# Sparse attention: keys and values multiplied once and copied to the other partitions by VectorE; compression's products alternate between TensorE's column groups

## The reference

```python
def nsa_mixer(h, w_in, w_out, pos_k, pos_v, k_w1, k_w2, v_w1, v_w2):   # G=4 groups, R=4 heads each, dh=64
    q, k_c, v_c, k_s, v_s, k_w, v_w, gates = jnp.split(h @ w_in, NSA_SPLITS, axis=-1)
    def compress(kv, pos, w1, w2):          # 15 windows of 32 tokens, stride 16
        blk = kv[:, cmp_idx] + pos[None, None, :, None, :]
        blk = jnp.moveaxis(blk, 3, 2).reshape(B_, n_cmp, G, CMP_BLOCK * dh)
        return jax.nn.gelu(blk @ w1) @ w2
    kc = compress(k_c, pos_k, k_w1, k_w2)
    vc = compress(v_c, pos_v, v_w1, v_w2)
    o_cmp = softmax(q kc) vc                # masked: windows that have ended
    o_slc = softmax(q k_s) v_s              # selected blocks: with 256 tokens all of them, causal
    o_win = softmax(q k_w) v_w              # window of 512: causal
    o = gates[0] * o_cmp + gates[1] * o_slc + gates[2] * o_win
    return o.reshape(B_, S_, NSA_HEADS * dh) @ w_out
```

## Time and profile before

| | |
|---|---|
| median of 3 runs | 3059.75 us (3054.98 to 3066.94) |
| the profiled execution | 3071.72 us, its span 3069.8 us |
| PE busy | 2931.2 us, 95% of the span |
| DVE busy | 2096.6 us, 68% |
| ACT busy | 1472.3 us, 48% |
| DMA | 521.48 MB, mean 170 GB/s |
| first sparse layer | its first unit begins at 1687.94 us, its attention ends at about 1854 us |
| second sparse layer | 2678.32 to about 2844 us |

### The profile page before, as it was taken

How to read it: one execution, slowest core, us unless ns; L and a number is a source line. 1 busy time by engine, 2 the same in 40 slices (tenths; PEclk the granted TensorE clock), 3 DMA queues, 4 the chain that set the end, 5 groups by cost and what they waited for, 6 DMA issues and landing times.

```text
span 3069.8 us, 54616 instructions
## 1 busy us (share of the span) xinstructions
PE 2931.2 (95%) x23236; PEld 2602.9 (85%) x23236; DVE 2096.6 (68%) x3263; ACT 1472.3 (48%) x1965; POOL 149.0 (5%) x257
## 2 busy tenths in 40 slices
PE   6999999989999998999999999999999999999998
PEld 5888899888888897998788878889788988897887
DVE  5976757668878776566775567754776677557674
ACT  2545544545445374445454355544554355435552
POOL 1000000200000000001000030000100000004000
PEclk9999999999999999999999999999999999999999
DMA  8875336448767642464564523554365555452452
GB/s 263 250 245 157 107 100 212 159 133 261 245 220 250 216 155 88 135 187 135 180 212 141 170 97 124 184 181 143 125 197 183 169 166 187 143 167 83 140 186 100
DMA packets 525026, 521.48 MB, mean 170 GB/s; under 512 B 16631, under 2 KB 522048, under 8 KB 524784
## 3 DMA queue, kind: packets, MB, share of 16 engines
q1 hardware_dynamic: 522176, 517.28, 52.8%
q0 software_dynamic: 816, 0.27, 0.1%
q10 hardware_dynamic: 1792, 0.44, 0.1%
HBM read 516.90 MB, written 1.05 MB: 169 GB/s over the span
## 4 chain that ended last, share of the span: by engine, by line
PE 83%; DVE 9%; ACT 5%; issue 2%; DMA 1%; POOL 0%; ACTq 0%; DVEq 0%; POOLq 0%; SPq 0%
PE P L65 82%; DVE wsp L74 4%; ACT wsp L71 2%; PE P L68 1%; ACT arena L71 1%; DVE ACC L82 1%; DVE arena L82 1%; DVE arena L74 1%; DVE X L74 1%; ACT L71 0%; ACT HX L71 0%; DVE HX L82 0%; DVE X L82 0%; DMA raw<-in_ada_w 0%; POOL arena L79 0%
## 5 line engine op out<-in xcount | busy, mean ns | idle before, releaser
L65 PE MATMUL P<-HX,wsp 128*128 128x512 f32 (+2 forms) x10688 | 1675.5, 319 | 33.1 <-DVE HX L82 11.9
L65 PEld LDWEIGHTS P<-HX,wsp 128*128 128x128 f32 (+1 forms) x10688 | 1510.3, 193 | 176.5 <-issue 13.8
L74 DVE TENSOR_TENSOR wsp<-raw,wsp 128x2048 fp32r<-128x2048 f32 (+3 forms) x448 | 964.7, 2155 | 388.6 <-ACT wsp L71 388.3
L71 ACT ACTIVATE wsp<-raw 128x2048 fp32r<-128x2048 f32 (+3 forms) x448 | 806.5, 1802 | 584.7 <-PE P L65 535.5
L65 PE MATMUL P<-FG,wsp 128*128 128x512 f32 (+1 forms) x2816 | 501.3, 340 | 1.2 <-DVE wsp L74 1.2
L65 PEld LDWEIGHTS P<-FG,wsp 128*128 128x128 f32 x2816 | 430.5, 188 | 67.0 <-DVE wsp L74 2.5
L71 ACT ACTIVATE arena<-P 128x512 f32<-128x512 f32 (+3 forms) x384 | 214.7, 569 | 560.8 <-PE P L65 559.9
L74 DVE TENSOR_TENSOR arena<-arena,P 128x512 f32<-128x512 f32 (+2 forms) x232 | 151.2, 653 | 196.8 <-ACT arena L71 163.4
L65 PE MATMUL P<-arena 64*64 64x64 f32 (+9 forms) x3936 | 246.5, 265 | 19.1 <-ACT arena L71 9.3
L65 PEld LDWEIGHTS P<-arena 64*64 64x64 f32 (+3 forms) x3936 | 196.3, 149 | 67.7 <-issue 32.6
L82 DVE SCALAR_TENSOR_TENSOR ACC<-raw,sm,ACC 128x256 f32<-128x256 f32 x476 | 230.8, 485 | 16.7
(11 more groups left out here) (110 smaller groups left out, 1394.7 us busy)
## 6 DMA issues: line engine op xcount, KB each, us to landing
raw<-in_ffn_w SPq DMA_DIRECT2D x120, 1024.0 KB, 5.4
raw<-in_ada_w SPq DMA_DIRECT2D x72, 1024.0 KB, 5.0
raw<-in_w_in SPq DMA_DIRECT2D x52, 1024.0 KB, 5.2
raw<-in_ffn_w_gate SPq DMA_DIRECT2D x44, 1024.0 KB, 5.3
raw<-in_ffn_w_up SPq DMA_DIRECT2D x44, 1024.0 KB, 5.3
raw<-in_ffn_w_down SPq DMA_DIRECT2D x32, 1024.0 KB, 5.1
raw<-in_ffn_w SPq DMA_DIRECT2D x16, 768.0 KB, 4.5
raw<-in_nsa_w_in SPq DMA_DIRECT2D x12, 1024.0 KB, 5.3
```

Of the source, the lines that this page charges most:

```text
L65: return self if self.e is None else self.e.matmul(*a, skip_group_check=True, **k)
L71: return self if self.e is None else self.e.activation(*a, **k)
L74: return self if self.e is None else self.e.tensor_tensor(*a)
```

## The change

The eight "dup" units of 128 columns become four plain units of 256: two `kvc` (all keys, all values) and two `kv` (all selected keys, all window keys). A plain unit leaves group 2m on partitions 0-63 and group 2m + 1 on 64-127. DVE, which evacuates PSUM with a multiplication anyway, writes each piece to the half where it is wanted: for `kvc` four writes of 64 partitions, two of them to the other half; for `kv` one write of 128 partitions in place and two of 64 partitions to the other half. The attention's key index follows.

The compression's products alternate, keys into partitions 0-63, values into 64-127. Its units are loaded in the order keys 0, values 0, keys 1, values 1, with q1 between the two pairs and q2 behind them, and PE multiplies in that order. The matmuls of `kc` alternate too. The compressed scores are made in products of 64 query positions instead of 128, alternating between PSUM's halves, and stand behind the first `kv` unit instead of ahead of it; DVE's and ACT's work on them moves with them, `q3` ahead of `kc`.

The diff, cut to its core:

```diff
             if kind == 0:
                 wi = A["nsa_w_in_2"][j]
-                cols(("kvc", j), wi, [128] * 4, 1024, "dup")
+                cols(("kvc", j), wi, w256 * 2, 1024)
                 cols(("gate", j), wi, [48], 2560)
                 cols(("q", j), wi, w256, 0)
-                for n in "kv":
-                    for s in range(2):
+                for s in range(2):
+                    for n in "kv":
                         unit(("cmp", j), A[f"nsa_cmp_{n}_w1_2"][j].rearrange("(k p) n -> p k n", p=128)[:, 8 * s:8 * s + 8, :], 8, 256, "raw")
-                cols(("q", j), wi, w256 * 3, 256)
+                    cols(("q", j), wi, w256, 256 + 256 * s)
+                cols(("q", j), wi, w256, 768)
                 for c in (1536, 2048):
-                    cols(("kv", j), wi, [128] * 2, c, "dup")
+                    cols(("kv", j), wi, w256, c)
                 for c in (1536, 2048):
                     cols(("kv", j), wi, w256, c + 256)
                 cols(("wo", 2 + i), A["nsa_w_out_2"][j], w256 * 4, 0)
@@ -2237,16 +2238,16 @@
             for h, br in ((2 * c + r, br) for c in range(8) for br in range(2) for r in range(2)):
                 g = h // 4
...
-                    opens=br == 0 and h % 2 == 0, last=br == 1 and h % 2 == 1, after=[kv_mark(j, 2 * br), kv_mark(j, 2 * br + 1)],
-                    v_after=[NAC.at((j, "ptc")), kv_mark(j, 4 + br)]))
+                    opens=br == 0 and h % 2 == 0, last=br == 1 and h % 2 == 1, after=[kv_mark(j, br)],
+                    v_after=[NAC.at((j, "ptc")), kv_mark(j, 2 + br)]))
...
-            for i in range(2):
-                e.wait_ge(*NVC.at((j, "kw", i)))
-                for s in range(2):
-                    u = U["cmp", j][2 * i + s]
-                    w = landed(u)
-                    e.wait_ge(*RAW[u % NR].at(u))
-                    for k in range(8):
-                        ins = e.matmul(P[b][64 * i:64 * i + 64, 0:256], KW[i][:, s, k, :, :].rearrange("p a b -> p (a b)"), w[:, k, :],
-                                       start=s == k == 0, stop=8 * s + k == 15)
-                    ins.then_inc(*MM.up(u))
+            for s in range(2):
+                us = [U["cmp", j][2 * s + i] for i in range(2)]
+                for i in range(2):
+                    e.wait_ge(*NVC.at((j, "kw", i)))
+                    e.wait_ge(*RAW[us[i] % NR].at(us[i]))
+                for k in range(8):
+                    for i in range(2):
+                        ins = e.matmul(P[b][64 * i:64 * i + 64, 0:256], KW[i][:, s, k, :, :].rearrange("p a b -> p (a b)"),
+                                       landed(us[i])[:, k, :], start=s == k == 0, stop=8 * s + k == 15)
+                        if k == 7:
+                            ins.then_inc(*MM.up(us[i]))
+                q_unit(1 + s)
             give(("cmp", j), NAC.at((j, "gelu")))
-            q_unit(1)
             b = take(e, ("hid", j))
             e.wait_ge(*NAC.at((j, "gelu")))
...
-            q_unit(2)
+            q_unit(3)
...
-            for r in range(2):
-                for k in range(2):
+            for k in range(2):
+                for r in range(2):
                     ins = e.matmul(P[b][64 * r:64 * r + 64, 0:64], W2[0][:, k, :], HID[:, k, 0, :], start=k == 0, stop=k == 1)
...
-            q_unit(3)
-            e.wait_ge(*NVC.at((j, "kc")))
...
-            for x in range(6):
+            for x in range(4):
                 u = U["kv", j][x]
                 b = take(e, ("kv", j, x))
-                if x < 4:
+                if x < 2:
                     ins = lin(e, u, b, hH, hL)
                 else:
                     ins = swapped(e, u, lambda t: P[b][:, 256 * t:256 * t + 256], hH, hL)
                 ins.then_inc(*MM.up(u))
                 give(("kv", j, x), kv_mark(j, x))
...
-                if x == 4:
+                if x == 0:
+                    e.wait_ge(*NVC.at((j, "kc")))
+                    e.wait_ge(*NVC.at((j, "q", 3)))
+                    for t in range(2):
+                        b = take(e, ("cs", j, t))
+                        for h2 in range(8):
+                            for y in range(2):
+                                ins = e.matmul(P[b][half(y), 32 * h2:32 * h2 + 32], Q[:, h2, 128 * t + 64 * y:128 * t + 64 * y + 64],
+                                               KCB[:, h2 // 2, :], start=True, stop=True)
+                        ins.then_inc(*NPE.up((j, "cs", t)))
+                        give(("cs", j, t), NVC.at((j, "s", t)))
...
-            for x in range(3):
+            for x in range(2):
                 ready_act(e, U["cmp", j][x])
+            ready_act(e, U["q", j][1])
+            ready_act(e, U["cmp", j][2])
             u = U["cmp", j][3]
             e.wait_ge(*MM.at(u))
             e.activation(HG, P[bank["cmp", j]][:, 0:256], ACT.Gelu_apprx_tanh).then_inc(*NAC.up((j, "gelu")))
             ready_act(e, u)
-            for i in range(1, 4):
+            for i in range(2, 4):
                 ready_act(e, U["q", j][i])
...
-                if x < 3:
+                if x == 0:
                     ready_act(e, u)
-                if x >= 4:
+                    for t in range(2):
+                        e.wait_ge(*NVC.at((j, "sub", t)))
+                        e.activation(v3(EC[:, t, :], 16), v3(SC[:, t, :], 16), ACT.Exp).then_inc(*NAC.up((j, "e", t)))
...
-            for x in range(4):
-                u = U["kvc", j][x]
-                i, gp = x // 2, x % 2
-                pv, r2 = v3(P[bank["kvc", j, x]][:, :], 2), R2
+            for i in range(2):
+                u = U["kvc", j][i]
+                pv, kb = v3(P[bank["kvc", j, i]][:, :], 2), KB[i].rearrange("p (m r) c -> p m r c", r=2)
                 e.wait_ge(*MM.at(u))
-                e.tensor_tensor(KB[i][0:64, 2 * gp:2 * gp + 2, :], pv[0:64], r2[0:64], ALU.mult)
-                e.tensor_tensor(KB[i][64:128, 2 * gp:2 * gp + 2, 0:255], pv[64:128, :, 1:256], r2[64:128, :, 1:256], ALU.mult).then_inc(*NVC.up((j, "kvc", x)))
+                for r in range(2):
+                    e.tensor_tensor(kb[0:64, :, r, :], pv[half(r)], R2[half(r)], ALU.mult)
+                    ins = e.tensor_tensor(kb[64:128, :, r, 0:255], pv[half(r), :, 1:256], R2[half(r), :, 1:256], ALU.mult)
+                ins.then_inc(*NVC.up((j, "kvc", i)))
                 ready_dve(e, u)
-                if x % 2:
-                    keys(i)
+                keys(i)
             ready_dve(e, U["gate", j][0])
             queries(0)
-            for x in range(4):
-                ready_dve(e, U["cmp", j][x])
-            queries(1)
+            for s in range(2):
+                for i in range(2):
+                    ready_dve(e, U["cmp", j][2 * s + i])
+                queries(1 + s)
...
-            for x in range(6):
+            for x in range(4):
                 u = U["kv", j][x]
-                if x < 4:
+                if x < 2:
+                    pv = v3(P[bank["kv", j, x]][:, :], 2)
                     e.wait_ge(*MM.at(u))
-                    e.tensor_tensor(KD_[x // 2][:, 2 * (x % 2):2 * (x % 2) + 2, :], v3(P[bank["kv", j, x]][:, :], 2), R2,
-                                    ALU.mult).then_inc(*NVC.up((j, "kv", x)))
-                if x < 3:
+                    e.tensor_tensor(KD_[x][:, 0:2, :], pv, R2, ALU.mult)
+                    for r in range(2):
+                        ins = e.tensor_tensor(KD_[x][half(1 - r), 2:4, :], pv[half(r)], R2[half(r)], ALU.mult)
+                    ins.then_inc(*NVC.up((j, "kv", x)))
+                if x == 0:
                     ready_dve(e, u)
-                if 1 <= x < 3:
-                    shares(x - 1)
-                if x >= 3:
-                    attend2_dve(e, 2 + 2 * j, jobs, 5120, 0.125, [x - 3])
+                    for t in range(2):
+                        scores(t)
+                    for t in range(2):
+                        shares(t)
+                if x >= 1:
+                    attend2_dve(e, 2 + 2 * j, jobs, 5120, 0.125, [x - 1])
```

More of the change, by code:

```diff
@@ L2312, in nsa_pe @@
             give(("vc", j), NVC.at((j, "vc")))
-            q_unit(3)
-            e.wait_ge(*NVC.at((j, "kc")))
-            e.wait_ge(*NVC.at((j, "q", 3)))
-            for t in range(2):
-                b = take(e, ("cs", j, t))
-                for h2 in range(8):
-                    ins = e.matmul(P[b][:, 32 * h2:32 * h2 + 32], Q[:, h2, 128 * t:128 * t + 128], KCB[:, h2 // 2, :], start=True, stop=True)
-                ins.then_inc(*NPE.up((j, "cs", t)))
-                give(("cs", j, t), NVC.at((j, "s", t)))
             jobs = nsa_jobs(j)
-            for x in range(6):
+            for x in range(4):
                 u = U["kv", j][x]
                 b = take(e, ("kv", j, x))
-                if x < 4:
+                if x < 2:
                     ins = lin(e, u, b, hH, hL)
@@ L2395, in keys @@
             def keys(i):
-                e.wait_ge(*NVC.at((j, "kvc", 2 * i + 1)))
```

(6 more changed lines are left out.)

29 lines of the change are left out of this document (13 added, 16 removed).

## The result

The changed kernel takes **3006.89 us**, median of 4 runs (3005.20 to 3012.29); before, in the same comparison, 3059.21 (4 runs, 3054.98 to 3066.94). The ratio is 0.982, 95% interval 0.9805 to 0.9836: 52 us less, faster by more than the 0.5% that can be told. Over all comparisons the changed kernel has 12 runs with median 3004.6 and the kernel before 29 with 3060.7. The forecast was 3005.

What follows compares the result with a forecast made beforehand. The prediction took TensorE's stream plus a few us of lost clock as the bound; terms summed to -27.4 us a layer, -54.8 for both, giving 3005 us against the median, range 2992 to 3020.

Steps and rivals of the forecast that it cites:

- (c): Compressed scores and second stage: narrower products at 0.064 us each, -0.2 us; idle ahead of scores gone, -0.9 us a layer.
- (e): TensorE's clock: drop after the scores goes, -2.6 us; same drop comes behind the new wait, +2.6; net 0 a layer.
- (a): TensorE's units: two compressed key/value and two selection/window units removed at 5.77 us each, -23.1 us a layer.
- (b): Compression: 64 records alternating output partitions go from 0.207 to 0.11 us each, -6.2 us a layer.
- (d): New TensorE wait ahead of the third query unit (q2), whose weight slot the compression's first half frees: +3.4 us a layer.
- (f): VectorE at the norm: TensorE no longer waits for a reciprocal held behind a subtraction, -0.4 us a layer.
- (g): VectorE before the compression: evacuations, subtractions and windows finish with 0.4 us to spare, so no wait, 0 us a layer.
- Rival D: Alternation saves nothing: compression keeps 13.2 us, the new wait is 0.3 us and its clock loss goes; 3006 us, chance 0.04.
- E: A case the prediction names without defining; its dear variant was left out of the range, no chance given.
- C: Another loss stays, the clock drop after the scores or late windows: +2.4 to 2.6 us a layer, 3010 us, chance 0.20.
- B: The clock stays up in the new wait, or the wait is shorter: -30.0 us a layer, 3000 us, chance 0.22.

Runs made afterwards that it cites:

- r2_serial: Changed kernel with each compression half doing the keys' eight products, then the values' eight, not alternating; 3001.26 us.
- r6_cs_wide: Changed kernel with compressed scores in products of 128 query positions as before the change, at their new place; 3010.07 us.
- r4_late: Changed kernel with q1 and q2 both between the compression's halves, second stage and scores one key unit later; 2994.70 us.
- r8_best: r4_late with q3's load ahead of the second half's loads and VectorE building the values' windows before splitting q1; 2993.97 us.
- r7_cs_serial: Changed kernel with the 64-wide score products not alternating: eight to one half of the output partitions, then eight to the other; 3003.11 us.
- r5_swap: Changed kernel with two loads exchanged, q2's ahead of the values' second compression unit; TensorE's order the same; 3008.64 us.
- r3_old_cmp: Changed kernel with the compression's product and load order as before the change, query units behind it; 2998.67 us.

## Why the prediction was right, point by point

The total was right, 3005 against 3006.9, and most terms held. That it came so close was in part luck: two terms, (c) and (e), were wrong to the same side, so that the two layers saved 60.4 us where 54.8 were forecast; the median moved by only 52.3. What took the difference lies outside the layers or in the scatter and stays open, as said at the end of this section.

| term, us per layer | forecast | measured, first layer |
|---|---|---|
| (a) units removed | -23.1 | -23.1: 192 records fewer, and the remaining units' price unchanged |
| (b) compression | -6.2 | -6.0: 13.2 became 3.6 + 3.6, 0.113 per record |
| (c) scores, idle ahead | -0.2, -0.9 | -2.2 (4.3 became 2.06), -0.9 |
| (d) new wait | +3.4 | +3.4 (second layer +3.0, see below) |
| (e) clock | 0 | -1.3: 2.7 gone, 1.4 back (2.6 in other executions: 0) |
| (f) spread | -0.4 | -0.4 |
| (g) VectorE | 0 | 0, and +0.6 or +0.7 in two of three executions |
| sum | -27.4 | -30.5; the layers' stretches say -30.1 and -30.3 |

**(a)** held, and is three quarters of the gain.

**(b)** held. The attention's row was the right price: 0.113 us per alternating record against 0.11. The Trainium skill (TensorE: Matmul & The Clock Gate, Part 3, The mechanism) has a weight load overlap a running product only where their row groups differ. The trace disagrees: the compression's products all use the same 128 rows, and they advance at 0.113 us per record when they alternate, less than a weight load's own 0.137, and at 0.19 in r2_serial's order. Alternating column groups alone was enough. Rival D's dear half and E fall with this.

**(c)** is the step that failed in size. "I take 0.064, what the 1-column records took" took a price from a stretch whose granted clock was 0.53; I had the clock in the same group of rows and did not take it into account. At full clock the same 16 records take 0.63 us, 0.04 each, and the scores measured 0.032. The 4.3 us of before were not at full clock either: in the trace of before their stretch had 0.86, and 0.79 in the second layer, where wide products at 1.00 take 3.50 us in r6_cs_wide. So some 0.6 us of the 2.2 are the clock's. The lower bound, 3.0 us for the stage, was too high as well, since it was half of a price of 64-column records.

**(d)** held to 0.1 us in the first layer, with its start 0.4 and its end 0.5 later than forecast. q2's weights were forecast 16.2 us after the start of the compression and PE began q2 after 16.67 (1720.13 to 1736.80), with the second block's end at 13.2 instead of 12.8. That the wait was nil before holds for the first layer alone: in the second, q1 had waited 0.42 us behind the compression, and the new wait there is 3.42. r2_serial, r4_late and r8_best confirm the chain: lengthen the block, or put another unit ahead, and the wait goes.

**(e)** was given as 0 from two equal losses. The old loss did go, and a loss did come with the wait, but of 1.4 us in both layers of the profiled execution. Over the executions of the changed kernel, and of r6_cs_wide and r7_cs_serial, which have the same wait, q2 took, with 3.3 to 3.5 us of idle ahead, 5.98 us once, 7.33 to 7.49 five times, and 8.49 to 8.60 three times: 0 to 2.6 lost. (The tenth, in r6_cs_wide, had 4.72 us of idle and lost 2.0.) The loss went together with an earlier one: it was least where the 120 records ahead of the compression had taken 14.5 us, most where 14.7, and 1.3 to 1.5 where 15.2 to 15.9. My account of the old loss was incomplete: I expected it to go because the idle of 0.87 us went, and r6_cs_wide lost 1.2 and 1.5 us without any. With narrow products, alternating or not, and no idle, none was lost; no run has narrow products behind an idle.

**(f)** held: no idle stands ahead of the spread at 1703.93.

**(g)** was a balance of 0.4 us, and it is as fine as that. DVE's timeline:

```profile
1712.34 2.79 DVE L74 TENSOR_TENSOR arena<-P,ACC 64x512 f32<-64x512 f32 x4
1715.16 2.29 DVE L74 TENSOR_TENSOR wsp<-raw,wsp 128x2048 fp32r<-128x2048 f32 x1
1717.37 2.26 DVE L74 TENSOR_TENSOR arena<-arena,PC 128x120 f32<-128x120 f32 x8
```

It ends at 1719.63, PE needs it at 1720.13. A write that goes to the other half of the partitions costs what one in place does: four take 2.79, 0.70 each, as in the earlier trace rows. Where the low clock near the norm lasts 1 us less (14.77 or 14.72 us for the 120 records instead of 15.73), PE is there first and waits 0.63 or 0.70. So part of what a better clock gives is taken back here. The GeLU was covered, as forecast: by 0.7 us in the profiled execution (made at 1743.4, PE there at 1744.1 after its slow q2) and by 0.3 in r7_cs_serial's second layer, where q2 ran at full clock. What I misread is where the cover of 0.2 came from: not from slack of ACT's but from the wait ahead of q2, and r5_swap turned it into a wait of 3.2.

**The rivals.** Rival D's remark, that the total can't tell it from the forecast, came true in another form: r2_serial and r3_old_cmp, which do without alternation, take the time of the changed kernel. C happened in a small way (late windows, 0.6 to 0.7 us where C had 2.4), B in one layer of r7_cs_serial.

**What stays open.** The layers say -60.4, the medians -52 to -59 (in the comparisons of the changed kernel itself 52.3, 56.9, 59.2 us), pooled -56. The rest of the span varied from 2722.4 to 2738.7 between profiled executions, most of it ahead of the first sparse layer, whose first unit began anywhere from 1676.84 to 1693.02; with a single profile of the kernel before, whether its rest is shorter by a few us cannot be told.

## What to carry to other kernels

A block that is made shorter uncovers what was loaded behind it: before an edit of this kind, count from the event that frees the slot through load, queue and splits, and move work between, or the gain comes back as a wait (here 12 us of 12). A step that is only just covered is not safe if what covers it is itself a wait: who removes that wait uncovers the step. And where totals scatter more than the effect, measure one stretch, between two fixed records, in every profile.

## What the runs showed of the hardware that I had not expected

- Products that alternate between column groups advance faster than one after another in the same group: 128 x 256 float32 records at 0.113 us against 0.19 to 0.207, 128 x 32 ones with 64 weight columns at 0.031 against 0.050; with 128 weight columns those take 0.109 at full clock.
- The granted clock can fall behind short products without any idle time: 32 records of 128 weight columns, in 3.98 and 3.66 us, were followed by stretches at 0.80 and 0.77; 64 records of 64 columns, in 2.06 or 3.30 us, were not.
- The same idle of 3.3 to 3.5 us between dense products was followed by no loss (once), by 1.3 to 1.5 us (five times) or by 2.5 to 2.6 (three times). The time of the 120 records ahead of the compression goes with it, as said under (e); the cause no run here shows.
- VectorE writes 64 x 512 results to the other half of the partitions at the price of the same half, 0.70 us.
